# Attention values of two heads in turn, and later reciprocals and turns, in a two-block transformer kernel on one Trainium2 core

## The reference

```
# latent attention, 8 heads, causal; q, k of 96 columns, v of 64
sc = einsum('bqhd,bkhd->bhqk', q, k) * 96 ** -0.5
sc = where(qpos[:, None] >= kpos[None, :], sc, -1e30)
o  = einsum('bhqk,bkhe->bqhe', softmax(sc), v)

# neighbourhood attention, 16 heads, q, k, v of 32 columns: each token attends to its
# window in the grid and to 256 context keys, 512 keys in all as the kernel lays them out
logits = concatenate([q @ k_window * scale + bias, q @ k_ctx * scale])
p = softmax(logits)
o = p_window @ v_window + p_ctx @ v_ctx
```

## Time and profile before

| | before |
|---|---|
| time, median of 3 runs | 2419.49 us (2415.57 to 2422.61) |
| the profiled execution's own time | 2422.61 us |
| its span, first to last instruction | 2421.1 us |
| PE busy | 2335.0 us (96%) |
| DVE busy | 1805.4 us (75%) |
| ACT busy | 1227.8 us (51%) |
| POOL busy | 413.4 us (17%) |
| mean granted TensorE clock | 0.986 of full |

### The profile page before, as it was taken

One profiled execution on the slowest core, in us unless ns is written; L12 is line 12 of the kernel. 1 busy time (PEld: TensorE's weight loads), 2 busy tenths in 40 slices (PEclk: granted clock), 3 DMA queues, 4 the chain that ended last, 5 costly groups with the idle time before them and its releaser, 6 DMA issues.

```text
span 2421.1 us, 27385 instructions
## 1 busy us (share of the span) xinstructions
PE 2335.0 (96%) x10949; PEld 1754.2 (72%) x10949; DVE 1805.4 (75%) x2024; ACT 1227.8 (51%) x1436; POOL 413.4 (17%) x447
## 2 busy tenths in 40 slices
PE   6987999999999999999999999999999999999998
PEld 2455897545599877455997578878887888788886
DVE  4855787687588854565665278888888888889897
ACT  1142653223255321233443277677777676777775
POOL 1243570134166010461320000000000000000000
PEclk9999999998999999899999999999999999999999
DMA  8632568651647874114665369999998999899995
GB/s 329 247 153 87 226 257 314 219 196 68 217 175 278 324 293 183 52 70 184 230 248 206 130 228 353 361 328 359 357 361 324 365 354 360 329 364 351 368 351 217
DMA packets 49462, 630.36 MB, mean 260 GB/s; under 512 B 7455, under 2 KB 8048, under 8 KB 11632
## 3 DMA queue, kind: packets, MB, share of 16 engines
q1 hardware_dynamic: 44192, 618.81, 67.9%
q10 hardware_dynamic: 2752, 6.99, 0.8%
q0 software_dynamic: 2384, 2.73, 0.3%
HBM read 624.83 MB, written 3.67 MB: 260 GB/s over the span
## 4 chain that ended last, share of the span: by engine, by line
PE 83%; DVE 9%; ACT 3%; DMA 2%; issue 2%; POOL 1%; SPq 0%; ACTq 0%; DVEq 0%
PE psum L1196 19%; PE psum L1197 19%; PE psum L1198 19%; PE psum L1062 5%; PE psum L1091 4%; PE psum L2613 3%; DVE sbuf L725 2%; PE psum L1280 2%; DVE ring_r L1191 2%; PE psum L1231 1%; PE psum L2616 1%; PE psum L3233 1%; DMA ring<-in_t_ada 1%; PE psum L2274 1%; DMA ring<-in_t_moe 1%
## 5 line engine op out<-in xcount | busy, mean ns | idle before, releaser
L1197 PE MATMUL psum<-ring_r,sc_r 128*128 128x512 f32 x1688 | 665.1, 394 | 0.0
L1191 DVE TENSOR_TENSOR ring_r<-ring,sbuf_r 128x2048 fp32r<-128x2048 f32 (+1 forms) x287 | 539.0, 1884 | 139.7 <-ACT sbuf_r L1182 138.1
L1182 ACT CAST sbuf_r<-ring 128x2048 fp32r<-128x2048 f32 (+1 forms) x287 | 446.4, 1558 | 314.8 <-PE psum L1198 256.8
L1191 DVE TENSOR_TENSOR ring_r<-ring,sc_r 128x2048 fp32r<-128x2048 f32 (+1 forms) x243 | 475.6, 1967 | 109.4 <-ACT sc_r L1182 108.6
L1182 ACT CAST sc_r<-ring 128x2048 fp32r<-128x2048 f32 (+1 forms) x243 | 398.6, 1644 | 243.8 <-PE psum L1198 216.0
L1196 PE MATMUL psum<-sbuf_r,sc_r 128*128 128x512 f32 (+1 forms) x1148 | 425.6, 371 | 3.6 <-DVE ring_r L1191 3.2
L1197 PEld LDWEIGHTS psum<-ring_r,sc_r 128*128 128x128 f32 x1688 | 316.9, 188 | 72.0 <-issue 1.4
L725 DVE SCALAR_TENSOR_TENSOR sbuf<-ring,sbuf 128x512 f32<-128x512 f32 x405 | 333.6, 831 | 14.1 <-DMA ring<-in_t_ada 8.5
L1198 PE MATMUL psum<-sbuf_r,sc_r 128*128 128x512 f32 x860 | 339.7, 395 | 0.0
L1196 PE MATMUL psum<-sc_r 128*128 128x512 f32 x828 | 331.1, 400 | 0.1
L1198 PE MATMUL psum<-sc_r 128*128 128x512 f32 x828 | 324.3, 392 | 0.0
(11 more groups left out here) (365 smaller groups left out, 2815.5 us busy)
## 6 DMA issues: line engine op xcount, KB each, us to landing
ring<-in_t_moe SPq DMA_DIRECT2D x168, 2048.0 KB, 7.9
ring<-in_t_ada SPq DMA_DIRECT2D x48, 2048.0 KB, 8.9
ring<-in_t_mlp SPq DMA_DIRECT2D x32, 2048.0 KB, 8.2
ring<-in_t_win SPq DMA_DIRECT2D x17, 2048.0 KB, 9.0
ring<-in_t_ffn SPq DMA_DIRECT2D x16, 2048.0 KB, 7.8
ring<-in_t_out SPq DMA_DIRECT2D x7, 2048.0 KB, 8.8
ring<-in_t_bias SPq DMA_DIRECT2D x2, 2048.0 KB, 8.3
spectra<-sc POOLq DMA_DIRECT2D x5, 512.0 KB, 3.7
```

The lines of the kernel that those rows point to most:

```text
L1182: p.act.e.copy(p.r(hi), src).then_inc(*p.sig("high", st.tag, n))
L1191: p.dve.e.tensor_tensor(p.r(src), src, p.r(hi), ALU.subtract).then_inc(*p.sig("lowp", st.tag, n))
L1197: e.matmul(out, l[0], r[1], start=False, stop=False)
```

## The change

Four edits.

1. `mla` and `na` get `pair=True` and four `PT` buffers instead of two; those that are added lie in memory that is idle then. `pe_values` does nothing for an even head; for an odd head the new `pe_pair_values` waits for all four jobs of the two heads and issues their products in turn: block 0 of head h - 1, block 0 of head h, block 1 of head h - 1, and so on.
2. `put_turned` waits for the values of head h - 4 instead of h - 2.
3. In `mla` the reciprocal of job i - 1 is taken in round i, behind `put_turned` and `put_values`; before, that of job i.
4. In `mla` PE issues the scores of a round ahead of the late transposition, and ACT does its exponential and its copies ahead of the copy of the late transposition. All late transpositions are waited for in round 8, ahead of its scores.

```
-        self.mla = mla = Heads("mla", [...], [xn[:, 512 * i:512 * i + 512] for i in range(2)], ..., 3, dil.DG)
+                               [xn[:, 512 * i:512 * i + 512] for i in range(4)], ..., 3, dil.DG, pair=True)
...
-        self.na = na = Heads("na", [...], [XN[:, i, :] for i in range(2)], ..., 3, late=1)
+                             [XN[:, 0, :], XN[:, 1, :], self.ht[:, 0:1024], self.acc[:, 0:1024]],
+                             ..., 3, late=1, pair=True)
...
 def pe_values(p, A, i):
     ...
+    if A.pair:
+        if j.head % 2:
+            pe_pair_values(p, A, j.head)
+        return
...
+def pe_pair_values(p, A, head):
+
+    pair = A.heads[head - 1], A.heads[head]
+    for q in A.of[head - 1] + A.of[head]:
+        p.pe.wait_ge(*p.at("pt" + A.side(A.jobs[q].nth), A.tag, A.jobs[q].nth))
+    if pair[0].opens:
+        for g in range(pair[0].group):
+            if group_bank(A, g) == pair[0].bank:
+                p.pe.wait_ge(*p.at("o" + A.side(g), A.tag, g))
+    n = len(pair[0].v)
+    for kb in range(n):
+        for h in pair:
+            q0 = 0 if (h.both or kb % 2 == 0) else 128
+            ins = p.pe.e.matmul(p.bank[h.bank][h.r0:h.r0 + h.v[kb].shape[1], q0:256], h.v[kb], h.pt[:, kb, q0:256],
+                                start=(kb == 0), stop=(kb == n - 1))
+            if kb == n - 1:
+                ins.then_inc(*p.sig("values", A.tag, h.index))
...
 def put_turned(p, E, side, A, i):
     ...
-    if j.head >= 2:
-        E.wait_ge(*p.at("values", A.tag, j.head - 2))
+    if j.head >= len(A.PT):
+        E.wait_ge(*p.at("values", A.tag, j.head - len(A.PT)))
...
-def dve_round(p, A, one, two, end):
+def dve_round(p, A, one, two, end, over=None):
     ...
-    if one is not None:
-        dve_over(p, A, one)
+    if over is None:
+        over = one
+    if over is not None and 0 <= over < len(A.jobs):
+        dve_over(p, A, over)
...
     for i, one, two, end in steps(p.mla):                  # pe_even
+        if i == 8:
+            for turn in LATE.values():
+                p.pe.wait_ge(*latent_at(p, turn))
+        if one is not None:
+            pe_scores(p, p.mla, one)
         if i in LATE:
             ...
             pe_latent(p, LATE[i])
-        if i in (8, 9):
-            for turn in LATE.values():
-                p.pe.wait_ge(*latent_at(p, turn))
-        pe_round(p, p.mla, one, two, end)
+        pe_round(p, p.mla, None, two, end)
...
     for i, one, two, end in steps(p.mla):                  # dve_even
-        dve_round(p, p.mla, one, two, end)
+        dve_round(p, p.mla, one, two, end, i - 1)
...
     for i, one, two, end in steps(p.mla):                  # act_even
+        act_round(p, p.mla, one, two, end)
         if i in LATE:
             put_latent(p, p.act, "A", LATE[i])
-        act_round(p, p.mla, one, two, end)
```

More of the change, by code:

```diff
@@ L503, in stages @@
         self.mla = mla = Heads("mla", [sc[:, 13824 + 256 * i:14080 + 256 * i] for i in range(4)],
-                               [xn[:, 512 * i:512 * i + 512] for i in range(2)], [(i,) for i in range(4)], [(4,), (5,)], 3,
-                               dil.DG)
+                               [xn[:, 512 * i:512 * i + 512] for i in range(4)], [(i,) for i in range(4)], [(4,), (5,)], 3,
+                               dil.DG, pair=True)
         for h in range(8):
-            mla.causal(self, h, h % 2, QT[0:96, h, :], KT[0:96, h, :])
-            mla.rows(h, 2, 64, [KV[:, k, 128 * h + 64:128 * h + 128] for k in range(2)], v3(mla.PT[h % 2], 2), [6, 7],
+            mla.causal(self, h, h % 4, QT[0:96, h, :], KT[0:96, h, :])
+            mla.rows(h, 2, 64, [KV[:, k, 128 * h + 64:128 * h + 128] for k in range(2)], v3(mla.PT[h % 4], 2), [6, 7],
                      HT[:, h // 2, :], False)
@@ L561, in stages @@
         self.SKIP = [KVC[:, o, 0:512] for o in range(2)]
-        self.na = na = Heads("na", [sc[:, 6168 + 512 * i:6680 + 512 * i] for i in range(4)], [XN[:, i, :] for i in range(2)],
-                             [(i,) for i in range(3)], [(3,), (4,)], 3, late=1)
+        self.na = na = Heads("na", [sc[:, 6168 + 512 * i:6680 + 512 * i] for i in range(4)],
+                             [XN[:, 0, :], XN[:, 1, :], self.ht[:, 0:1024], self.acc[:, 0:1024]],
+                             [(i,) for i in range(3)], [(3,), (4,)], 3, late=1, pair=True)
         for h in range(16):
-            pt = v3(na.PT[h % 2], 4)
+            pt = v3(na.PT[h % 4], 4)
             r0 = 32 * (h % 4)
@@ L638, with __init__ @@
 class Heads:
-    def __init__(self, tag, P, PT, s_banks, t_banks, depth, DG=(), late=0):
+    def __init__(self, tag, P, PT, s_banks, t_banks, depth, DG=(), late=0, pair=False):
         self.tag, self.P, self.PT, self.s_banks, self.t_banks, self.depth = tag, P, PT, s_banks, t_banks, depth
-        self.DG, self.late = DG, late
+        self.DG, self.late, self.pair = DG, late, pair
         self.jobs, self.heads, self.groups, self.turned = [], [], 0, []
```

## The result

| | before | after |
|---|---|---|
| time, median | 2416.48 us of 6 runs (2415.36 to 2422.61) | 2400.06 us of 6 runs (2395.83 to 2402.84) |
| ratio after to before | | 0.9926, 95% interval 0.9913 to 0.9940 |
| the profiled execution's own time | 2422.61 us | 2402.84 us |
| its span | 2421.1 us | 2401.5 us |
| mean granted TensorE clock | 0.986 | 0.986 |

By the ratio the changed kernel is faster by 0.74%. The kernel before came out at 2416.48 in these six runs, three of which are those behind the median of 2419.49 against which the forecast was set. In a later set, five more runs of the changed kernel had a median of 2403.05 and a ratio of 0.9942 (0.9929 to 0.9956).

The account below looks back on a forecast made before the run. TensorE was taken to bound neighbourhood attention, VectorE to pace latent attention. Savings of 13.0 and 0.5 us made 13.5, so 2406.0 us from a median of 2419.49, range 2403.5 to 2420.5.

Parts of the forecast that it names:

- What bounds the kernel: TensorE bounds the neighbourhood attention; in the latent attention VectorE sets the pace, idle 7.0 us before 14 reciprocals.
- Part 1: Neighbourhood attention: values of two heads in turn overlap, a pair costs 2.06 us, not 3.68; eight save 13.0.
- VectorE as next bound: Neighbourhood attention: VectorE's 10.7 us stays below TensorE's new period of 11.42, about 0.7 left; TensorE narrowly remains the bound.
- Part 2: Latent attention: four terms, taken together as 0.5 us of gain, with -3 to +2 as bounds.
- (b): Latent attention: late transpositions keep rounds 3 to 6 at some 1.8 us; round 7's maximum comes at 204.5, not 204.93.
- (c): Latent attention, rounds 7 to 15: they go at the pace of (a); job 15's maximum starts 3.1 us earlier.
- (a): Latent attention: the reciprocal's wait goes, at most 7.0 us; round 3 to 15 without waits is 18.4, now 23.55.
- (d): Latent attention's end: last reciprocal about 221.0, end 224.7 or 225.1, not 226.25; a low clock would return 0.5 to 2.
- The sum: Whole kernel: 13.0 from neighbourhood and 0.5 from latent attention, 13.5 us less, 2406.0 on the median.
- Serial passes: Rival: TensorE runs passes in order whatever their columns; neighbourhood gains 1.0, latent about 0.5, time 2418; chance 0.20.
- partial overlap: Rival: weight loads set the pace or VectorE becomes the bound in neighbourhood attention; 2410 to 2415 us; chance 0.13.
- a change of tile that empties the array: Rival: in neighbourhood attention each tile change waits for the last result, 9 to 16 us more, 2428 to 2436; chance 0.12.

Follow-up runs that it names:

- `na_pair_only`: The kernel before with the paired values in the neighbourhood attention alone, latent attention as before: 2407.65 us, ratio 0.9957.
- `same_columns`: The changed kernel, but in neighbourhood attention a pair's second head uses the first's 32 columns, its result left out of the output: 2419.31 us, ratio 1.0005.

## Why the prediction was right and wrong

**What bounds the kernel.** Right. A TensorE microsecond taken from the neighbourhood attention came through, and the latent attention moved with VectorE's wait.

**Part 1.** The mechanism was right, and the step that was mis-sized is the pair: nine slots and 2.06 us were forecast, eight and 1.85 were measured. The first pass of the second head starts with that of the first, not one slot later. That would make the term 14.6 instead of 13.0. The stage gave 12.9 in the first two traces and 10.8 in the mean of six and six. What is missing is a term that the sum did not have here: the clock, with 8.5 us more at the 1.2 GHz level on average. It dips once in the steady part of the stage of the first trace and three times in that of `na_pair_only`, although TensorE is not idle there, and for longer near the stage's start in all six. That 10.8 is as near to 13.0 as it is, is luck: a pair that saves more and a clock that takes more of it back. The Trainium skill, "TensorE: Matmul & The Clock Gate", part 3 (its span model), says that products in different tiles together last as long as one, plus some 4 ns for each further tile. By it, as an estimate, a pair is 4 x 0.434 + 0.12 = 1.86 us, and the trace agrees with 1.85 and with starts 6 or 7 ns apart; I should have weighed that sentence and not the factor for three tiles beside it (by which, as an estimate, a pair is 3.68 / (2 x 0.79) = 2.33 and eight save 10.8, not the 11.5 of the prediction). The same part's rule that a weight load passes a running product only with another row group would have kept the loads apart; 16 loads on the same rows fit into 1.85 us, most of them started 1 or 2 ns behind a pass of 0.379, so the trace speaks against it here. In the latent attention eight loads of 0.137, 1.1 us one after the other, fit into 0.87.

**VectorE as next bound.** This was right. Its slack was forecast at 0.7 us in a period, where it waited 1.85 before the convolution's part. In the two steady periods with that part it now waits 0.69 and 0.43 us (last in brackets):

```profile
1037.23 0.69 DVE L2770 TENSOR_TENSOR sc<-psum,sc 128x512 f32<-128x512 f32 x1 [0.69 <-PE psum L2744]
...
1048.41 0.69 DVE L2770 TENSOR_TENSOR sc<-psum,sc 128x512 f32<-128x512 f32 x1 [0.43 <-PE psum L2744]
```

The two other waits on that line, 1.93 and 3.04 us, lie at the stage's start behind convolution steps at the low clock. TensorE stayed the bound, narrowly. With four heads in turn the fear came true.

**Part 2.** This is where the forecast was wrong, and of the terms for changed lines the one that promised too little (0.5 us, where the stage gave 2.9). The step that failed is (b): "Nearly all of the gain of these rounds is lost", to the late transpositions. From the first maximum to that of job 7 it took 11.18 instead of 13.42, where some 13 was forecast. I had worked out rounds 3 to 6 at 1.8 each, and there (b) was right, they took 7.45 in all, 1.86 each; but rounds 0 to 2 came 1.9 us sooner (3.73 instead of 5.62), which the working had not counted. (c) inherited the error and added 1.5 of its own: it has 13.1 us from the maximum of job 7 to that of job 15, where the rounds of (a) with two second products add up to 12.4 and the trace took 11.58. The rounds were priced too high; without waits an even one takes 1.05 and an odd one 1.37, not 1.17 and 1.46. Against the bound of (a), 18.4 us from job 3 to job 15, it took 19.03. The last maximum, counted from the first, is 6.4 us sooner and not 3.1. (d) held in its sum, not in its parts: from the last maximum to the projection 7.6 us, where 225.1 less 217.6 makes 7.5, but the last reciprocal came after 2.96 instead of 3.4, and from it to the projection 4.62 instead of 4.1. There the low clock cost more than the 0.5 to 2 forecast: 1.5 on the projection, and some 1.2 on the last turn (1.22 where (d) has 0.66) and the last pair (1.55 where one at the full clock took 0.87). The stage gained 2.9 in the first trace instead of 0.5, and 2.7 as a kernel of its own. Of the edits it is the late reciprocal alone that is shown to gain; the pairs, though they overlap fully there too, bring the latent attention nothing that can be told.

**The sum.** Forecast -13.5. The profile has -12.9 and -2.9, and 3.7 in stretches that no edit touches. Without that and with the stage means it is -10.8 and -2.9: about what was forecast, but by luck, through two errors of opposite sign, 2.2 too much and 2.4 too little. The range was too narrow downwards, since it held no term for the swing of unchanged stretches, which is as large as its distance to the forecast (2.5), nor for the median of three runs on which it was set, which came out 3.0 lower over six.

**The rivals.** Serial passes are excluded by 1.85 against 3.57 on the same columns; partial overlap exists, but here only when the heads go one after the other (2.74); a change of tile that empties the array is excluded by the same 1.85.

## What to carry to other kernels

Small products that use different columns of the array take the time of one when they are issued in turn, so look in the chain for runs of products with few stationary columns that bound a stage, and put the next head's between them; issued head after head, half of the gain of each step is gone, and of the stage's 10.8 us one trace kept 2.4. Read the granted clock beside every stage that is made denser or that is left waiting, since it can take back a quarter of what the denser order saves (some 3.8 of 14.6 us here). Count the buffers before more heads are taken together. Read one stage in several traces of the same code before a microsecond in it is put down to an edit: here identical code differed by 1.3 us in the latent attention. And when a reciprocal or another small step waits for an engine that comes later, move it a round back first, which is the cheap part and here gained most of its stage.

## What the hardware did that I had not expected

- Two column tiles of 128 x 32 in plain float32 lie fully over each other (16 passes in 1.85 us, 8 in 1.84), and four nearly so (32 in 1.93).
- The overlap reaches over several instructions: with four products of one head ahead of four of the other, four of sixteen passes were still covered (2.74 us), and the second head's first pass started ahead of the first head's last three.
- The loads of different columns lie over each other too: eight of 0.137 us in a run of 0.87.
- The granted clock fell to 0.50 in stretches in which TensorE's row is busy without a gap (1068 to 1070 us after, 1024 to 1026 us with pairs in the neighbourhood attention alone), and its mean over the stage was 0.94 to 0.97 without pairs, 0.90 to 0.93 with two heads in turn, 0.76 to 0.81 with four. The last figure includes gaps of TensorE. That the denser order causes the lower clock is not shown: with all passes serial and the row full it also fell, at 1016 us of `same_columns`.
- Stretches with identical code differ between executions by several us: the first maximum of the latent attention came at 188.5 to 193.5 us, and the stretch from the end of that stage to the neighbourhood attention took 735.0 to 740.8.
